# Two side places for pieces of expert 0, and decay pre-activations from complete low-rank sums in four 32-row groups

## What is computed

```python
# decay of the gated linear attention: a low-rank product, then a bias, then a log-sigmoid
la_f = log_sigmoid((p[..., OFF_AF:OFF_AF + 16] @ wa2_f) + ba_f) / 16.0      # p = h @ w_in
la_b = log_sigmoid((p[..., OFF_AB:OFF_AB + 16] @ wa2_b) + ba_b) / 16.0

# expert-choice routing, 16 experts, 64 sample slots and 16 prompt slots each
gates, idx = top_k(softmax(x @ router_w).T, cap)
xe = x[idx]
h = silu(xe @ w1[e]) * (xe @ w3[e])        # 1024 -> 2048, per expert
ye = (h @ w2[e]) * gates                   # 2048 -> 1024
out = zeros.at[idx].add(ye)
```

## Time and profile before

| | |
|---|---|
| median of three runs | 1336.98 us (1335.88 to 1337.0) |
| the profiled execution's own time | 1337.34 us |
| its span | 1335.5 us |
| TensorE busy (PE) | 1319.6 us, 99% |
| VectorE, ScalarE, GpSimd busy | 462.4, 170.5, 109.4 us |
| mean granted TensorE clock | 0.994 of full |
| DMA over the span | 353 GB/s; from slice 12 of 40 on, 408 to 431 GB/s |

### The profile page before, as it was taken

The page is one execution under the profiler, slowest core; times in us unless marked ns, Lnnn a source line. Parts: engine busy times, 40 slices in busy tenths (PEclk is TensorE's granted clock), DMA queues, the critical chain, the costliest instruction groups (busy, mean ns, idle before and its releaser), DMA issues.

```text
span 1335.5 us, 24267 instructions
## 1 busy us (share of the span) xinstructions
PE 1319.6 (99%) x10761; PEld 469.9 (35%) x10761; DVE 462.4 (35%) x850; ACT 170.5 (13%) x277; POOL 109.4 (8%) x119
## 2 busy tenths in 40 slices
PE   8999999999999999999999999999999999999997
PEld 3544555554333333333333333333333333333332
DVE  3189886977130403122121214041221212130405
ACT  3443624123100000000000000000000000000002
POOL 0300000110110101010000001010101000000000
PEclk8999999999999999999999999999999999999999
DMA  9733731247799999999999999999999999999996
GB/s 315 254 126 134 252 118 34 78 159 287 285 425 419 424 420 414 431 415 431 415 427 419 427 420 426 420 423 422 415 430 416 428 418 427 420 425 421 427 408 248
DMA packets 64350, 470.88 MB, mean 353 GB/s; under 512 B 5686, under 2 KB 17795, under 8 KB 39739
## 3 DMA queue, kind: packets, MB, share of 16 engines
q1 hardware_dynamic: 57184, 451.56, 81.6%
q0 software_dynamic: 6320, 18.45, 4.5%
q10 hardware_dynamic: 810, 0.37, 0.1%
HBM read 456.99 MB, written 13.37 MB: 352 GB/s over the span
## 4 chain that ended last, share of the span: by engine, by line
PE 94%; DMA 2%; DVE 1%; SPq 1%; issue 1%; ACT 0%; POOLq 0%; POOL 0%; DVEq 0%
PE psum L1273 48%; PE psum L1289 16%; PE psum L1300 8%; PE psum L843 8%; PE psum L1117 4%; PE psum L885 2%; PE psum L1059 2%; DMA ring<-in_exp_w_dram 2%; PE psum L930 1%; PE psum L1069 1%; SPq L578 1%; DMA ring<-in_ada_w_dram 1%; PE psum L786 0%; PE psum L1023 0%; PE psum L1028 0%
## 5 line engine op out<-in xcount | busy, mean ns | idle before, releaser
L1273 PE MATMUL psum<-ring,both 128*32 128x512 f32 x6144 | 664.6, 593 | 0.6 <-issue 0.6
L1273 PEld LDWEIGHTS psum<-ring,both 128*32 128x32 f32 x6144 | 199.4, 110 | 457.5 <-issue 457.3
L2206 DVE TENSOR_TENSOR both<-both,psum 128x512 f32<-128x512 f32 x48 | 50.3, 1049 | 555.7 <-PE psum L1273 555.7
L1289 PE MATMUL psum<-ring,both 128*32 128x512 f32 x2048 | 231.3, 592 | 0.0
L1627 ACT ACTIVATE both<-psum 128x512 f32<-128x512 f32 x48 | 28.7, 597 | 934.0 <-PE psum L1273 934.0
L1289 PEld LDWEIGHTS psum<-ring,both 128*32 128x32 f32 x2048 | 66.6, 110 | 153.2 <-issue 153.2
L1300 PE MATMUL psum<-ring,both 128*32 128x512 f32 x1024 | 118.7, 592 | 0.1
L843 PE MATMUL psum<-ring,feat 128*128 128x512 f32 x240 | 104.3, 593 | 0.0
L701 POOL DMA_INDIRECT both<-xn_dram,both x45 | 49.5, 1100 | 579.3 <-DVE both L2217 569.8
L2236 DVE SCALAR_TENSOR_TENSOR both<-psum,both 64x512 f32<-64x512 f32 x32 | 24.0, 750 | 178.1 <-PE psum L1300 177.9
L1117 PE MATMUL psum<-ring,both 128*128 128x512 f32 x160 | 71.2, 596 | 0.0
(11 more groups left out here) (312 smaller groups left out, 627.7 us busy)
## 6 DMA issues: line engine op xcount, KB each, us to landing
ring<-in_exp_w_dram SPq DMA_DIRECT2D x192, 2048.0 KB, 17.9
ring<-in_ada_w_dram SPq DMA_DIRECT2D x8, 2048.0 KB, 7.9
ring<-in_w_in_dram SPq DMA_DIRECT2D x4, 2048.0 KB, 11.1
ring<-in_ada_w_dram SPq DMA_DIRECT2D x6, 1024.0 KB, 11.6
ring<-in_w_out_dram SPq DMA_DIRECT2D x2, 2048.0 KB, 10.0
acc_dram<-x POOLq DMA_DIRECT2D x5, 512.0 KB, 3.0
xn_dram<-feat POOLq DMA_DIRECT2D x5, 512.0 KB, 5.7
x<-acc_dram SPq DMA_DIRECT2D x5, 512.0 KB, 18.1
```

What stands on the lines that cost most here:

```text
L1273: mm = nc.tensor.matmul(role_bank(role)[f4 * PART:(f4 + 1) * PART, :], xe[:, kt, part * PART:(part + 1) * PART], w[:, kt % 2, f4 * 512:(f4 ...
L1289: mm = nc.tensor.matmul(role_bank("Y_A")[at:at + PART, :], h[:, c, part * PART:(part + 1) * PART], w[:, f, half * 512:(half + 1) * 512], s ...
L2206: role_stored(nc.vector.tensor_tensor(h_rows[:, part, :].rearrange("p (c a) -> p a c", a=PART), silu_h[:, part % 2, :].rearrange("p (a c) ...
```

## The change

**Side places.** Pieces 6 and 7 of expert 0 no longer go to ring slots 3 and 4 but to the storage of the sample tiles of `x` and of `feat`, which have been saved to DRAM by then. The order of issue becomes 0, 1, 2, 3, 4, 6, 5, 7, 8 to 11. The wait on `gathered` moves from piece 4 to piece 5; piece 6 waits for the saves of `x`, the last sample tile's norm and its turn; piece 7 waits for the saves of `xn2`. Pieces 8 to 11 go to the slots of pieces 0 to 3, and the first two pieces of expert 1 to those of pieces 4 and 5; from there on all pieces keep a distance of six. GpSimd waits for the saves of `x` before the gather too.

**Decay stage.** "aS" becomes 32 products of 128 tokens: token tile t goes to output rows 32t to 32t+31, summed over all eight k-blocks, so each group holds a complete sum of one tile. "zS" becomes 16 products over 32 rows: row group t times head, each row group with a bank of its own. TensorE waits for "aS" alone before them and for "aP" only before "zP". `aT` shrinks to 256 columns. VectorE adds the bias with five instructions of 128x512 with a broadcast operand.

```diff
+SIDE = {6: "x_rows", 7: "xn2_rows"}
+FIRST_ORDER = [0, 1, 2, 3, 4, 6, 5, 7, 8, 9, 10, 11]
+def place_of(m, expert):
+    turn = m if expert == 0 and m < RING else m - len(SIDE) if expert == 0 else m + EXPERT_LOADS - len(SIDE)
+    return EXPERT_SLOT[turn % RING]
...
+        side = {6: x_rows[:, 0:CHUNK_F], 7: feat[:, 0:CHUNK_F]}
...
             wait_filled(sp, JOB["o", TILES - 1])
             sp.wait_ge(o_ready, TILES)
-            for m in range(RING):
-                if m >= 3:
+            for m in FIRST_ORDER:
+                if m == 6:
+                    sp.wait_ge(acc_saved, 16 * ST)
+                    sp.wait_ge(xn2_ready, ST)
+                    wait_filled(sp, JOB["hT", ST - 1, 1])
+                elif m == 7:
+                    sp.wait_ge(xn2_saved, 16 * ST)
+                elif m >= 8:
+                    wait_expert_chunk_read(sp, m - 8, 0)
+                elif m >= 3:
                     wait_trunk_chunk_read(sp, chunk_before(EXPERT_SLOT[m], len(TRUNK_CHUNKS)))
-                if m == 4:
+                if m == 5:
                     sp.wait_ge(gathered, 16)
-                load_expert_chunk(m, 0)
-            for m in range(RING, EXPERT_LOADS):
-                wait_expert_chunk_read(sp, m - RING, 0)
-                load_expert_chunk(m, 0)
-            with sp.Fori(1, LAST) as expert:
+                load_expert_chunk(m, 0, first=True)
+            for m in range(EXPERT_LOADS):
+                if m < 2:
+                    wait_expert_chunk_read(sp, m + 4, 0)
+                else:
+                    wait_expert_chunk_read(sp, m - RING, 1)
+                load_expert_chunk(m, 1)
+            with sp.Fori(2, LAST) as expert:
...
             pool.wait_ge(xn2_saved, 16 * ST)
+            pool.wait_ge(acc_saved, 16 * ST)
             wait_stored(pool, JOB["slotsS",])
...
-            for name, lo, hi in (("aS", 0, SAMPLE), ("aP", SAMPLE, TOK)):
...
+            n = JOB["aS",]
+            wait_bank_free(pe, n)
+            for kt in range(KT):
+                for t in range(ST):
+                    mm = nc.tensor.matmul(bank(n)[t * PART:(t + 1) * PART, 0:P], w_a[:, kt, :], hT[:, kt, t * P:(t + 1) * P],
+                                          start=(kt == 0), stop=(kt == KT - 1))
+            filled(mm, n)
...
             wait_stored(pe, JOB["aS",])
+            for t in range(ST):
+                wait_bank_free(pe, JOB["zS", t])
+            for hd in range(HEADS):
+                for t in range(ST):
+                    n, rows = JOB["zS", t], slice(t * PART, (t + 1) * PART)
+                    mm = nc.tensor.matmul(bank(n)[:, hd * P:(hd + 1) * P], a_up[rows, hd, :], aT[rows, 0:P], start=True, stop=True)
+                    if hd == HEADS - 1:
+                        filled(mm, n)
             wait_stored(pe, JOB["aP",])
-            for hd in range(HEADS):
-                n = JOB["zS", hd]
-                wait_bank_free(pe, n)
-                filled(nc.tensor.matmul(bank(n), a_up[:, hd, :], aT[:, 0:SAMPLE], start=True, stop=True), n)
...
-            for hd in range(HEADS):
-                n = JOB["zS", hd]
-                wait_filled(dve, n)
-                stored(nc.vector.tensor_scalar(z3[:, hd, 0:SAMPLE], bank(n), vecs[:, V_BA + hd:V_BA + hd + 1], None, ALU.add), n)
...
+            for t in range(TILES):
+                n = JOB["zS", t] if t < ST else JOB["zP",]
                 wait_filled(dve, n)
+                stored(nc.vector.tensor_tensor(z3[:, :, t * P:(t + 1) * P], bank(n).rearrange("p (h n) -> p h n", h=HEADS),
+                                               vecs[:, V_BA:V_BA + HEADS, None].to_broadcast([P, HEADS, P]), ALU.add), n)
```

More of the change, by code:

```diff
@@ L192, with loads_before @@
 EXPERT_SLOT = [3, 4, 5, 2, 0, 1]
-LOADS_BEFORE = [CHUNK_SLOT.count(s) for s in range(RING)]
 EXPERT_LOADS = 12
+SIDE = {6: "x_rows", 7: "xn2_rows"}
[3 more added lines that the diff above has]
+    return EXPERT_SLOT[turn % RING]
+def loads_before(m, expert):
+    slot = place_of(m, expert)
+    first = [place_of(i, 0) for i in range(EXPERT_LOADS) if i not in SIDE and (expert > 0 or i < m)]
+    own = [place_of(i, 1) for i in range(m)] if expert > 0 else []
+    return CHUNK_SLOT.count(slot) + first.count(slot) + own.count(slot)
 def trunk_kernel(nc, x_prompt, x_sample, s0_f, s0_b, c, c_ctx, ada_w, ada_b, norm1_w, w_in, wa2_f, ba_f,
@@ L586, in _, with load_expert_chunk @@
                     .then_inc(qk_pair_loaded[c] if c < PAIRS - 1 else slot_loaded[2], 16)
-            def load_expert_chunk(m, expert):
-                slot = EXPERT_SLOT[m % RING]
+            def load_expert_chunk(m, expert, first=False):
+                slot = place_of(m, 0 if first else 1)
+                place, loaded = (side[m], side_loaded[m]) if first and m in SIDE else (chunk(slot), slot_loaded[slot])
                 if m < 8:
@@ L958, in _ @@
             for hd in range(HEADS):
[L959 removed]
+                mm = nc.tensor.matmul(bank(n)[:, hd * P:(hd + 1) * P], a_up[:, hd, :], aT[:, P:2 * P], start=True, stop=True)
             filled(mm, n)
@@ L1279, in up_chunk @@
                 def up_chunk(which, k2):
-                    return wait_expert_chunk(pe, EXPERT_CHUNKS.index((which, k2)), expert).rearrange("p (k n) -> p k n", k=2)
+                    return wait_expert_chunk(pe, EXPERT_CHUNKS.index((which, k2)), expert, first).rearrange("p (k n) -> p k n", k=2)
                 def down_sample(i, w):
@@ L1304, in down_chunk @@
                 def down_chunk(i):
-                    return wait_expert_chunk(pe, 8 + i, expert).rearrange("p (k n) -> p k n", k=4)
+                    return wait_expert_chunk(pe, 8 + i, expert, first).rearrange("p (k n) -> p k n", k=4)
                 if not first:
```

52 lines of the change are left out of this document (28 added, 24 removed).

## The result

The changed kernel takes 1340.62 us (median of 8 executions, 1337.63 to 1342.46) against 1336.99 (1335.13 to 1338.34): ratio 1.0027, 95% interval 1.0017 to 1.0036. The forecast of 1336.0 and its range up to 1339.8 were too low. Slower it is in both; by 2 or by 3.6 us depends on the session, and so does whether the range held. The profiled execution took 1340.65 us.

A forecast was written before the change was run, and what follows sets the result against it. TensorE's own path was taken as the bound, through decay stage and handover, not weight loads. Decay -2.2, gather +1.5, end -0.3 gave -1.0 us: 1336.0 us against the median, range 1332.8 to 1339.8, the forecast's own 1334.2 to 1338.2.

The forecast's parts named there:

- Decay stage: Low-rank products before the v projection: v would start at 73.55 instead of 75.74 us, a gain of 2.2 us.
- rival 3: Decay stage: row groups do not overlap, gain 0.6 us in place of 2.2, time 1337.6 us; chance 0.07.
- So the 2.2 us should reach the handover: Between decay stage and experts: no new TensorE wait from 76 to 320 us, so all 2.2 us arrive.
- Rival 4: Before the handover: the decay gain is lost since VectorE moved less, time 1338.2 us; chance 0.09.
- Price of the gather: Handover to the experts: the gather takes 5.5 us beside early loads, +1.5 us, bounds 0 and +4.2.
- Clock "no change": Start of the experts: the half-clock stretch, costing 1.7 us, stays as it was; bounds -1.7 and +1.7 us.
- End: Last w2 products: loads run ahead, so the wait for weights at 1313 us goes, -0.3 us.
- Rival 2: Handover: gather starved and last save late, +3.2 us, 1340.2 us, or 1341.9 with a second slow clock stretch; chance 0.12.

The follow-up runs named there:

- e1: The kernel before with the decay change alone, no side places: 1335.8 us, ratio 0.9995.
- e10: The kernel before with 36 products of 32 columns added in the first 10 us: 1351.15 us, ratio 1.0107.
- e13: The decay change alone, plus 100 waits on a long-set semaphore between the v and g products: 1334.56 us, ratio 0.998 against the kernel before.
- e17: The changed kernel with the wait for the gathered rows moved behind piece 5, so pieces 4, 6 and 5 go ahead of the gather: 1343.81 us, ratio 1.0046.
- e3: The changed kernel once more, unaltered, in a later session: 1338.94 us, ratio 1.0015.
- e8: The changed kernel with four spare products before TensorE's wait for the gathered rows: 1337.29 us, ratio 1.0002.
- e7: The decay change alone, with four products of 32 columns added in the first 10 us: 1337.09 us, ratio 0.9994.
- e4: The kernel before once more, unchanged: 1336.99 us, ratio 1.0002.
- e16: The kernel before with one more spare product before the top tokens' rows wait and one of 256 columns before the gathered rows wait: 1335.5 us, ratio 0.9993.

## Why the prediction missed

- **Decay stage: right.** Forecast 2.2 us, measured 2.09. "zS" took 37 ns for each instruction (1.17 us for 32) against the 29 taken, and "zP" waited for ScalarE's copies, as foreseen. Row groups overlap: rival 3 did not happen, nor did the 3.4 us of loads in series that the prediction worked out from the Trainium skill's price.
- **"So the 2.2 us should reach the handover": failed.** I looked for waits on VectorE between 76 and 320 us and for none on DMA. The wait for U had 0.3 us to spare, and I did not compute it. `e1`, `e10` and `e13` show what used it up: a code packet in the load, 0.3 to 0.7 us of wait. Rival 4 has the right kind of loss with the wrong cause.
- **Price of the gather: too small, and it brings the next miss with it.** I took 5.5 us because "the loads drain in its middle"; it was 6.1 to 6.5, so +2.1 to +2.6 in place of +1.5. The drain time was right (330 to 334, measured 332). Wrong was that the gather would progress beside the loads at 84 GB/s: it moved next to nothing until they ended, and then waited for one engine that ended the loads 1.7 us and more after the rest. With even engines it would have taken about 5.4 us by estimate, near the 5.5 of the sum although the overlap was wrong; that is chance. The row of 8.2 us for gathers beside loads should have weighed more than the mean of the ends.
- **Clock "no change": failed, and by size the largest miss.** Of the kernels with a wait of 0.7 us, four of nine profiled executions have the slow stretch; with 2.8 us and more all three, once twice as long, and `e17` three times. A cost that the old kernel paid in a part of its executions became certain: 1.65 us of median (`e3` less `e8`). In a profile the stretch costs 1.1 to 1.9 us up to the first w2 product (45.8 us in the changed kernel and 46.3 in `e7`, against 44.7 in `e8` and 44.4 in `e13`). I compared with the one profile of before, which had the stretch, and so could see no loss in it.
- **End: -0.26 as forecast, for another reason.** `e1` and `e7`, without side places, have it too (5.33 us for 48 w2 instructions, as in the changed kernel), and the kernel before had 0.17 of it in `e4`. `e16` and `e10`, with loads and decay stage as before, have all of it. So it is scatter, and the side places are not shown to bring any.
- **Rival 2** came closest in its number (gather starved, slow clock stretch again, 1340.2 to 1341.9), and in part by luck: it needed +4.2 for the gather and a late save. The gather cost +2.1 to +2.6, and the save landed at 326.03, before the gather's issue. I gave it 0.12 because "the loads run out"; they ran out 3 us after the gather's issue, which was late enough.

With what was measured: -2.1 + 0.5 (U) + 2.3 (gather) + 1.0 (clock: a part of the executions newly slow, and some twice as long) = +1.7 us, which fits `e3` (+2.0). The 1.0 is an estimate, not a measurement; with the 1.65 of `e3` less `e8` in its place the sum is +2.3. Against the forecast of -1.0 this is 1.0 for the clock, 0.8 for the gather, 0.5 for the U load, 0.3 for the end and 0.1 for the decay stage. Of the first session's +3.6 the rest, some 1.9 us, is not explained. The start of its profile suggests the scatter of the first 70 us (1.3 us of a late load and 1.6 of half clock); `e17` has the same late start. That makes two of the ten profiles with the new decay stage and no products added at the start, and none of the four with the old one. That the change makes it more frequent is neither shown nor excluded.

One sum of the prediction does not come out: with the gather between 0 and +4.2 the forecast's own range is 1334.5 to 1338.7, and not 1334.2 to 1338.2. It changes nothing here.

## What to carry to other kernels

Loads that are moved into an empty stretch must leave free the time of the small transfer on which the path hangs, and its neighbours: check the issue times of every small transfer against the drain time of the loads ahead, and let no large load be in flight at the issue. A transfer ends with its slowest engine, so one late engine is enough. Judge a gain by the slack of each load that is issued on the same path, not only by the waits that are there: 0.3 us of slack before the U weights was not visible as a wait. And take the clock from several executions: one profile shows one draw of it.

The version to keep is `e13`: the decay stage in four row groups with the code packets out of the U load, no side places, 2.3 us below the kernel before.

## What the runs showed of the hardware

- A 16 KB packet of code on one DMA engine lengthens a 2 MB load by 1.1 us (9.0 against 7.9): fifteen engines close the U load by 7.5 us and the one with the packet at 8.0 to 8.4. Adding instructions moves these packets through the program.
- Where a 2 MB load and a small gather share the engines they take turns about one packet for one, whatever the size: 79 packets of 16 KB against 73 of the gather in `e17`. The gather then gets a fifth of the bytes of the load (0.26 against 1.28 MB).
- A gather issued behind 4 MB of loads closed on fifteen engines by 4.5 us and landed only at 6.13, after the engine that ended the loads last.
- Small products are not cheap where their weights are wide. The products of `e10`, with 128x128 weights and 32 moving columns, took 111 ns each at the full clock (36 in 4.00 us) and 205 ns at half, with the weight loads busy all the time:

```profile
5.00:9.00 4.00, 4.00 (x36) 4.00 (x34) 0.00 (x0) 0.88 (x2) 0.00 (x0) 1.00 1.00 392
9.00:17.00 8.00, 8.00 (x39) 8.00 (x38) 0.00 (x0) 0.00 (x0) 0.00 (x0) 0.50 1.16 306
```

- The 111 ns are near what the Trainium skill states for a load of 128 columns, P / 1.2, that is 107 ns (page "TensorE: Matmul & The Clock Gate", section "LDWEIGHTS (loading the stationary operand)"); the 205 ns at half clock are not in that price. Nor is it the distance between starts where the loads go to different row groups: 37 ns each in "zS".
- Waits on a semaphore that is already set cost the array nothing between long products: with 100 more instructions in v and g it was 69.34 us against 69.33.
